# The order of the root, the rounding of the first weight tile and the turns in the normalisations of a two-layer hybrid block

## The chip, the cores and the metric

The kernel runs on one core of one Trainium2 chip. The metric is the time of one execution on the device in microseconds (us). Engines are TensorE (PE, and PEld for its weight loads), VectorE (DVE), ScalarE (ACT), GpSimd (POOL) and SyncE (SP, which issues most transfers).

## The reference

The program computes two layers of a backbone over 512 latent tokens and, as a prefix, 256 context tokens of width 1024. A layer is a token mixer (differential attention, a 2-D Fourier branch and a bidirectional RWKV-7 scan, fed by one input projection, merged by gates) and a channel mixer (ConvGLU). Each of the two begins with a plain layer norm that is then modulated, and its result is multiplied by a weight matrix:

```python
def _ln_plain(x):
    xf = x.astype(jnp.float32)
    mu = jnp.mean(xf, axis=-1, keepdims=True)
    var = jnp.mean(jnp.square(xf - mu), axis=-1, keepdims=True)
    return ((xf - mu) * lax.rsqrt(var + LN_EPS)).astype(x.dtype)

def _modulate(x, shift, scale):
    return _ln_plain(x) * (1.0 + scale) + shift
...
P = _in_proj(_modulate(x, mod[0], mod[1]), ...)           # h @ w_in
f = _conv_ffn(_modulate(x, mod[3], mod[4]), lp)           # u, g = split(h @ ffn_up)
```

The last layer does not need the context tokens in its channel mixer.

## The kernel before

The stream x stays in SBUF, token-major: 128 tokens on the partitions, 1024 features along them, 6 token tiles (4 latent, 2 context). The program is a sequence of stages, each with one instruction list per engine and a barrier at its end; engines order themselves by semaphores within a stage. Products are done in float32 with both operands split in two parts: "hi", the value rounded to the matmul's format, and "lo", the remainder. A product adds hi x hi, hi x lo and lo x hi. Weight tiles of 1024 x 128 (512 KB) are loaded by SyncE into a ring of three (`load_weights`, L312), rounded by ScalarE (`split_hi`, L319, the activation is L325), and their remainder is taken by GpSimd (`split_lo`, L327, L331). SyncE loads tile n when the remainder of tile n - 3 is done.

`norm` (L348) is part of four stages: ahead of the input projection of layer 0 and layer 1 (called from L441: the first and the third normalisation), and ahead of the channel mixer of layer 0 and layer 1 (called from L2134: the second and the fourth). The first three have 6 token tiles, the fourth has 4. It works like this:

- VectorE aggregates the statistics of each token tile (L369; in the first normalisation it takes the statistics themselves too, L364) and adds epsilon (L372). ScalarE takes the root (L400), VectorE the reciprocal (L374) and the product `neg_mean` = -mean/std (L376).
- The rows are normalised token tile by token tile: tiles 0, 1, 3, 4 by VectorE (L378), tiles 2 and 5 by ScalarE (L403). With four tiles these are 0, 1, 3 and 2.
- TensorE turns (transposes) the normalised rows in blocks of 128 x 128 (L393). For feature block j = 0 to 7 it turns this block of all token tiles, into one of three pairs of PSUM banks, and signals `n_T`. It begins when all token tiles are normalised; from block 3 on it waits until the pair of banks has been read.
- ScalarE scales and shifts a turned block out of PSUM (L409, one instruction for the latent and one for the context tokens), from block 3 on when the remainder of block j - 3 is done. GpSimd rounds it (the cast, L417) and VectorE takes the remainder (L382).

Each engine does this ahead of its own part of the stage. The very first things in ScalarE's and GpSimd's lists are the rounding and the remainder of weight tile 0:

```python
            def _(act):
                split_hi(act, sem, rings, 0)
                act.wait_ge(sem("n_var"), 1)
                act.activation(rs[:, 0:nt], rs[:, 0:nt], ACT.Sqrt).then_inc(sem("n_std"), 1)
...
            def _(pool):
                split_lo(pool, sem, rings, 0)
```

After the eight blocks ScalarE rounds weight tile 1 and GpSimd takes its remainder. TensorE, behind its last turn, multiplies weight tile 0 by the activations (`fm_product`, L334, the matmul is L340): for each of the 8 blocks of 128 features three products, of 512 and 256 columns with six tiles and of 512 with four, each block waiting for its remainder (`n_lo`). All further products follow. In the channel mixer two later weight tiles have their remainder taken by VectorE (L2367).

Of the kernel before, what the change touches and what calls it, by code (L numbers as in the profile page):

```python
# [133 lines left out]
def program(nc, A, out):  # L134
    with ExitStack() as top:
# [212 lines left out]
        def norm(sc, block, sem, l, i_shift, i_scale, nt, h, xn, hf, rings, counted):  # L348
# [11 lines left out]
            @block.vector  # L360
            def _(dve):
                for t in range(0 if counted else nt):
                    for f in range(2):
                        i = dve.bn_stats(st_x[:, t, f, :], x[:, t, f * 512:(f + 1) * 512])  # L364
                    i.then_inc(sem("n_stats"), 1)
                for t in range(nt):
                    if not counted:
                        dve.wait_ge(sem("n_stats"), t + 1)
                    i = dve.bn_aggr(mv[:, t, :], st_x[:, t, :, :])  # L369
                i.then_inc(sem("n_mv"), 1)  # L370
                dve.wait_ge(sem("n_mv"), 1)
                dve.tensor_scalar(rs[:, 0:nt], mv[:, 0:nt, 1], LN_EPS, None, ALU.add).then_inc(sem("n_var"), 1)  # L372
                dve.wait_ge(sem("n_std"), 1)
                dve.reciprocal(rs[:, 0:nt], rs[:, 0:nt]).then_inc(sem("n_rstd"), 1)  # L374
                dve.wait_ge(sem("n_rstd"), 1)
                dve.scalar_tensor_tensor(nb[:, 0:nt], mv[:, 0:nt, 0], -1.0, rs[:, 0:nt], ALU.mult, ALU.mult).then_inc(sem("n_nb"), 1)  # L376
                for t in by_dve:
                    dve.tensor_scalar(xn[:, t, :], x[:, t, :], mv[:, t, 0:1], rs[:, t:t + 1],  # L378
                                      ALU.subtract, ALU.mult).then_inc(sem("n_xn"), 1)
                for j in range(KT):  # L380
                    dve.wait_ge(sem("n_hi"), j + 1)
                    dve.tensor_tensor(h[1][:, j, 0:n_tok], hf[:, j % 3, 0:n_tok], h[0][:, j, 0:n_tok].bitcast(F32),  # L382
                                      ALU.subtract).then_inc(sem("n_lo"), 1)

            @block.tensor
            def _(pe):
                pe.wait_ge(sem("n_xn"), len(by_dve))
                pe.wait_ge(sem("n_xa"), len(by_act))
                for j in range(KT):
                    if j >= 3:  # L390
                        pe.wait_ge(sem("n_h"), j - 2)
                    for t in range(nt):
                        m = pe.transpose(bank(2 + 2 * (j % 3), P, t * P), xn[:, t, j * P:(j + 1) * P], ident[:, :])  # L393
                    m.then_inc(sem("n_T"), 1)

            @block.scalar
            def _(act):
                split_hi(act, sem, rings, 0)
                act.wait_ge(sem("n_var"), 1)
                act.activation(rs[:, 0:nt], rs[:, 0:nt], ACT.Sqrt).then_inc(sem("n_std"), 1)  # L400
                act.wait_ge(sem("n_nb"), 1)
                for t in by_act:
                    act.activation(xn[:, t, :], x[:, t, :], ACT.Identity, bias=nb[:, t:t + 1], scale=rs[:, t:t + 1]).then_inc(sem("n_xa"), 1)  # L403
                for j in range(KT):
                    act.wait_ge(sem("n_T"), j + 1)
                    if j >= 3:
                        act.wait_ge(sem("n_lo"), j - 2)
                    for s, (at, n) in enumerate(BOTH if ctx else LAT):
                        m = act.activation(hf[:, j % 3, at:at + n], bank(2 + 2 * (j % 3), n, at), ACT.Identity, bias=sh(j, s), scale=sl(j, s))  # L409
                    m.then_inc(sem("n_h"), 1)  # L410

            @block.gpsimd
            def _(pool):
                split_lo(pool, sem, rings, 0)
                for j in range(KT):
                    pool.wait_ge(sem("n_h"), j + 1)
                    pool.tensor_copy(h[0][:, j, 0:n_tok], hf[:, j % 3, 0:n_tok]).then_inc(sem("n_hi"), 1)  # L417
# [2009 lines left out]
```

## Time and profile before

| | us |
|---|---|
| median of 3 runs | 3760.12 |
| the three runs | 3756.68, 3760.12, 3762.56 |
| the profiled execution, its own time | 3761.08 |
| its span (first to last instruction) | 3758.9 |

TensorE is busy for 3436.3 us of the span, VectorE 1561.3, ScalarE 1263.3 and GpSimd 1081.2; the granted TensorE clock is 0.965 of full speed on average. All starts in the rows below are microseconds from the start of the span. The second column of a timeline row is the time from the start of the first to the end of the last of the instructions merged in it (x4 means four of them); what stands in brackets is the engine's idle time before it and whose signal ended it.

### The profile page before, as it was taken

How to read it: one execution, taken by the hardware profiler on the slowest of the kernel's cores; microseconds unless marked ns; L12 is line 12 of the kernel's file. 1: busy time of each engine (PE TensorE's matmuls, PEld its weight loads, DVE VectorE, ACT ScalarE, POOL GpSimd, SP SyncE). 2: the span in 40 equal slices, each digit the busy share in tenths (PEclk: the TensorE clock that was granted, in tenths of full speed). 3: DMA queues.
4: the chain of work that ended last, by engine and by line, in shares of the span. 5: the costliest groups of instructions: out<-in, count | busy, mean ns of one | idle time of the engine just before them, and what ended most of it. 6: DMA issues, size and time to landing. Idle time of an engine off the chain costs nothing. (4 is left out here: it accounts for less than half of the span.)

```text
span 3758.9 us, 82172 instructions
## 1 busy us (share of the span) xinstructions
PE 3436.3 (91%) x36724; PEld 2756.7 (73%) x36724; DVE 1561.3 (42%) x2341; ACT 1263.3 (34%) x2064; POOL 1081.2 (29%) x649
## 2 busy tenths in 40 slices
PE   5989999999888999799999898999999898969998
PEld 3658888888655777687878666888888666558887
DVE  3233344333177645622112634344443376362224
ACT  3322243333255423221222143234333365223222
POOL 2211132232111412233333232123333113235553
PEclk8989999999999999899999999999999999989999
DMA  6663323342221433133332145334442323433332
GB/s 225 227 196 110 106 77 114 114 127 85 84 85 37 158 115 128 45 129 113 122 119 96 39 144 170 96 109 123 124 121 83 104 90 116 144 95 101 95 96 89
DMA packets 444248, 427.58 MB, mean 114 GB/s; under 512 B 15540, under 2 KB 369002, under 8 KB 436986
## 3 DMA queue, kind: packets, MB, share of 16 engines
q1 hardware_dynamic: 442314, 413.55, 34.9%
q10 hardware_dynamic: 1584, 8.78, 0.6%
q8 instruction: 290, 4.75, 0.5%
q14 instruction: 60, 0.49, 0.0%
HBM read 333.54 MB, written 88.74 MB: 112 GB/s over the span
## 5 line engine op out<-in xcount | busy, mean ns | idle before, releaser
L857 PE MATMUL ps<-I-281_h_hi,I-284_w_hi 128*128 128x256 f32 (+1 forms) x832 | 298.4, 359 | 14.2 <-ACT I-1974_result L1063 9.7
L857 PE MATMUL ps<-I-281_h_hi,I-285_w_lo 128*128 128x256 f32 (+1 forms) x832 | 282.6, 340 | 2.7 <-issue 2.7
L857 PE MATMUL ps<-I-282_h_lo,I-284_w_hi 128*128 128x256 f32 (+1 forms) x832 | 282.9, 340 | 0.0
L2286 POOL TENSOR_TENSOR I-18334_w_lo<-I-18332_w_raw,I-18333_w_hi 128x1024 fp32r<-128x1024 f32 x60 | 145.0, 2416 | 342.5 <-ACT I-18333_w_hi L2249 342.4
L857 PE MATMUL ps<-I-23080_h_hi,I-23083_w_hi 128*128 128x512 f32 (+1 forms) x544 | 213.2, 392 | 13.4 <-ACT I-24473_result L1063 7.8
L857 PE MATMUL ps<-I-23081_h_lo,I-23083_w_hi 128*128 128x512 f32 (+1 forms) x544 | 201.3, 370 | 0.0
L857 PE MATMUL ps<-I-23080_h_hi,I-23084_w_lo 128*128 128x512 f32 (+1 forms) x544 | 200.9, 369 | 0.0
L2286 POOL TENSOR_TENSOR I-38121_w_lo<-I-38119_w_raw,I-38120_w_hi 128x1024 fp32r<-128x1024 f32 x60 | 144.2, 2404 | 154.4 <-ACT I-38120_w_hi L2249 154.4
L857 PEld LDWEIGHTS ps<-I-281_h_hi,I-284_w_hi 128*128 128x128 f32 x832 | 158.8, 191 | 39.0 <-ACT I-1974_result L1063 9.9
L340 PE MATMUL ps<-I-18329_h_hi,I-18333_w_hi 128*128 128x512 f32 x704 | 183.1, 341 | 1.0 <-DVE I-18330_h_lo L382 1.0
L821 POOL TENSOR_TENSOR I-285_w_lo<-I-283_w_raw,I-284_w_hi 128x1024 fp32r<-128x1024 f32 x34 | 82.3, 2421 | 353.4 <-ACT I-284_w_hi L1081 353.4
L2249 ACT ACTIVATE I-18333_w_hi<-I-18332_w_raw 128x1024 fp32r<-128x1024 f32 x61 | 64.6, 1059 | 354.7 <-PE ps L340 234.9
L340 PE MATMUL ps<-I-18329_h_hi,I-18334_w_lo 128*128 128x512 f32 x704 | 182.1, 340 | 0.0
L340 PE MATMUL ps<-I-18330_h_lo,I-18333_w_hi 128*128 128x512 f32 x704 | 180.1, 337 | 0.0
L857 PEld LDWEIGHTS ps<-I-281_h_hi,I-285_w_lo 128*128 128x128 f32 x832 | 159.0, 191 | 17.7
L821 POOL TENSOR_TENSOR I-23084_w_lo<-I-23082_w_raw,I-23083_w_hi 128x1024 fp32r<-128x1024 f32 x34 | 84.8, 2494 | 297.0 <-ACT I-23083_w_hi L1081 297.0
L857 PEld LDWEIGHTS ps<-I-282_h_lo,I-284_w_hi 128*128 128x128 f32 x832 | 159.3, 191 | 14.2
L1063 ACT ACTIVATE I-1974_result<-ps 128x512 f32<-128x512 f32 x104 | 51.1, 493 | 340.1 <-PE ps L857 340.0
L340 PE MATMUL ps<-I-38116_h_hi,I-38120_w_hi 128*128 128x512 f32 x352 | 137.6, 391 | 1.8 <-DVE I-38117_h_lo L382 1.8
L340 PE MATMUL ps<-I-38116_h_hi,I-38121_w_lo 128*128 128x512 f32 x352 | 137.0, 389 | 0.0
L340 PE MATMUL ps<-I-38117_h_lo,I-38120_w_hi 128*128 128x512 f32 x352 | 137.0, 389 | 0.0
L918 PEld LDWEIGHTS ps<-I-49_x 64*64 64x64 f32 x3840 | 116.8, 135 | 21.6 <-issue 12.6
(892 smaller groups left out, 8826.3 us busy)
## 6 DMA issues: line engine op xcount, KB each, us to landing
I-283_w_raw<-in_w_in SPq DMA_DIRECT2D x67, 512.0 KB, 6.1
I-23082_w_raw<-in_w_in SPq DMA_DIRECT2D x67, 512.0 KB, 5.1
I-18342_ada_w<-in_ada_w SPq DMA_DIRECT2D x24, 1024.0 KB, 5.9
I-18332_w_raw<-in_ffn_up SPq DMA_DIRECT2D x44, 512.0 KB, 3.9
I-38119_w_raw<-in_ffn_up SPq DMA_DIRECT2D x44, 512.0 KB, 3.9
proj_d<-I-1974_result SPq DMA_DIRECT2D x52, 384.0 KB, 2.8
I-482_ada_w<-in_ada_w SPq DMA_DIRECT2D x16, 1024.0 KB, 5.6
I-18332_w_raw<-in_ffn_down SPq DMA_DIRECT2D x22, 512.0 KB, 3.3
```

Of the source, the lines that this page charges most:

```text
L340: m = pe.matmul(dst[:, at:at + n], w[wi][:, k, :], a[ai][:, k, at:at + n], start=k == 0 and i == 0, stop=k == kt - 1 and i == 2)
L821: pool.tensor_tensor(lo(s), raw(s), hi(s).bitcast(F32), ALU.subtract).then_inc(sem("w_lo"), 1)
L857: m = pe.matmul(bank(6 + i % 2, n_c), w[:, k, :], hv[:, k, c0:c0 + n_c], start=k == 0 and v == 0, stop=k == KT - 1 and v == 2)
L918: m = pe.matmul(side(ps[rows(i), (4 + d) * 512 + c0:(4 + d) * 512 + c0 + C], n_lv, d), NAT[d][rows(1 - i), c0:c0 + C], side(T[d][rows(1 - ...
L1063: act.activation(res[:, s % 2, c0:c0 + n_c], bank(6 + i % 2, n_c), ACT.Copy, scale=DH_A ** -0.5 if J_Q <= slots[s][0] < J_K else 1.0).then ...
L2249: act.activation(pair(g)[0], rings[0][:, g % 3, :, :], ACT.Copy).then_inc(sem("w_hi"), 1)
L2286: pool.tensor_tensor(pair(g)[1], rings[0][:, g % 3, :, :], pair(g)[0].bitcast(F32), ALU.subtract).then_inc(sem("w_lo"), 1)
```

## The change

In `norm`, ScalarE takes the root and normalises its token tiles first, and rounds weight tile 0 after that. The remainder of weight tile 0 moves from the head of GpSimd's list to VectorE's, behind its normalised rows and ahead of the remainders of the activations. TensorE turns the first three feature blocks token tile by token tile (tile 0, 2, 1, 5, 3, 4 with six tiles; 0, 2, 1, 3 with four), waiting for each tile by itself, and signals the three blocks with the turns of the last token tile; blocks 3 to 7 are turned as before.

```diff
@@ -377,6 +377,7 @@
                 for t in by_dve:
                     dve.tensor_scalar(xn[:, t, :], x[:, t, :], mv[:, t, 0:1], rs[:, t:t + 1],
                                       ALU.subtract, ALU.mult).then_inc(sem("n_xn"), 1)
+                split_lo(dve, sem, rings, 0)
                 for j in range(KT):
                     dve.wait_ge(sem("n_hi"), j + 1)
                     dve.tensor_tensor(h[1][:, j, 0:n_tok], hf[:, j % 3, 0:n_tok], h[0][:, j, 0:n_tok].bitcast(F32),
@@ -384,23 +385,31 @@
 
             @block.tensor
             def _(pe):
-                pe.wait_ge(sem("n_xn"), len(by_dve))
-                pe.wait_ge(sem("n_xa"), len(by_act))
-                for j in range(KT):
-                    if j >= 3:
-                        pe.wait_ge(sem("n_h"), j - 2)
+                turn = lambda j, t: pe.transpose(bank(2 + 2 * (j % 3), P, t * P), xn[:, t, j * P:(j + 1) * P], ident[:, :])
+                order = sorted(range(nt), key=lambda t: (by_act if t in by_act else by_dve).index(t))
+                for t in order:
+                    if t in by_act:
+                        pe.wait_ge(sem("n_xa"), by_act.index(t) + 1)
+                    else:
+                        pe.wait_ge(sem("n_xn"), by_dve.index(t) + 1)
+                    for j in range(3):
+                        m = turn(j, t)
+                        if t == order[-1]:
+                            m.then_inc(sem("n_T"), 1)
+                for j in range(3, KT):
+                    pe.wait_ge(sem("n_h"), j - 2)
                     for t in range(nt):
-                        m = pe.transpose(bank(2 + 2 * (j % 3), P, t * P), xn[:, t, j * P:(j + 1) * P], ident[:, :])
+                        m = turn(j, t)
                     m.then_inc(sem("n_T"), 1)
 
             @block.scalar
             def _(act):
-                split_hi(act, sem, rings, 0)
                 act.wait_ge(sem("n_var"), 1)
                 act.activation(rs[:, 0:nt], rs[:, 0:nt], ACT.Sqrt).then_inc(sem("n_std"), 1)
                 act.wait_ge(sem("n_nb"), 1)
                 for t in by_act:
                     act.activation(xn[:, t, :], x[:, t, :], ACT.Identity, bias=nb[:, t:t + 1], scale=rs[:, t:t + 1]).then_inc(sem("n_xa"), 1)
+                split_hi(act, sem, rings, 0)
                 for j in range(KT):
                     act.wait_ge(sem("n_T"), j + 1)
                     if j >= 3:
@@ -411,7 +420,6 @@
 
             @block.gpsimd
             def _(pool):
-                split_lo(pool, sem, rings, 0)
                 for j in range(KT):
                     pool.wait_ge(sem("n_h"), j + 1)
                     pool.tensor_copy(h[0][:, j, 0:n_tok], hf[:, j % 3, 0:n_tok]).then_inc(sem("n_hi"), 1)
```

## Rows read from the trace of the kernel before

**Rows 1.** The page, part 1: busy time, share of the span, instructions.

```profile
PE 3436.3 (91%) x36724; PEld 2756.7 (73%) x36724; DVE 1561.3 (42%) x2341; ACT 1263.3 (34%) x2064; POOL 1081.2 (29%) x649
```

**Rows 2.** The chain that ended last: start, duration (us), what.

```profile
3371.60 1.06 ACT I-38120_w_hi L325
...
3372.99 2.09 DVE I-38136_neg_mean L376
...
3390.43 11.86 PE ps L340 x51
```

**Rows 3.** Timeline of ScalarE, second normalisation: start, duration, what, [idle before <- releaser].

```profile
1543.46 1.06 ACT L325 ACTIVATE I-18333_w_hi<-I-18332_w_raw 128x1024 fp32r<-128x1024 f32 x1 [8.76 <-DMA I-18332_w_raw<-in_ffn_up]
...
1546.99 2.37 ACT L403 ACTIVATE I-18336_x_norm<-I-49_x,I-18350_neg_mean,I-18349_rstd 128x1024 f32<-128x1024 f32 x2 [2.37 <-DVE I-18350_neg_mean L376]
1551.48 4.76 ACT L409 ACTIVATE I-18337_h_f<-ps,I-63_mod 128x512 f32<-128x512 f32 x8 [2.12 <-PE ps L393]
```

**Rows 4.** Timeline of VectorE, second normalisation.

```profile
1539.94 0.17 DVE L372 TENSOR_SCALAR I-18349_rstd<-I-18348_mean_var 128x6 f32<-128x6 f32 x1
...
1544.88 2.08 DVE L376 SCALAR_TENSOR_TENSOR I-18350_neg_mean<-I-18348_mean_var,I-18349_rstd 128x6 f32<-128x6 f32 x1
1546.88 2.97 DVE L378 TENSOR_SCALAR I-18336_x_norm<-I-49_x,I-18348_mean_var,I-18349_rstd 128x1024 f32<-128x1024 f32 x4
```

**Rows 5.** Timeline of GpSimd, second normalisation.

```profile
1544.60 2.34 POOL L331 TENSOR_TENSOR I-18334_w_lo<-I-18332_w_raw,I-18333_w_hi 128x1024 fp32r<-128x1024 f32 x1 [47.83 <-ACT I-18333_w_hi L325]
```

**Rows 6.** Timeline of TensorE, second normalisation.

```profile
1549.90 6.15 PE L393 MATMUL ps<-I-50_ident,I-18336_x_norm 128*128 128x128 f32 x36 [23.80 <-DVE I-18336_x_norm L378]
```

**Rows 7.** Timelines of ScalarE, then VectorE, first normalisation.

```profile
46.37 1.28 ACT L400 ACT_TABLE_LOAD   x1
...
54.28 6.20 ACT L409 ACTIVATE I-290_rv_raw<-ps,I-63_mod 128x512 f32<-128x512 f32 x10 [2.12 <-PE ps L393]
...
48.92 0.17 DVE L372 TENSOR_SCALAR I-298_rstd<-I-297_mean_var 128x6 f32<-128x6 f32 x1
...
49.59 0.17 DVE L376 SCALAR_TENSOR_TENSOR I-299_neg_mean<-I-297_mean_var,I-298_rstd 128x6 f32<-128x6 f32 x1
49.67 2.97 DVE L378 TENSOR_SCALAR I-287_k_and_kk<-I-49_x,I-297_mean_var,I-298_rstd 128x1024 f32<-128x1024 f32 x4
```

**Rows 8.** Timelines of ScalarE, then VectorE, third normalisation.

```profile
2161.33 1.06 ACT L325 ACTIVATE I-23083_w_hi<-I-23082_w_raw 128x1024 fp32r<-128x1024 f32 x1 [9.12 <-DMA I-23082_w_raw<-in_w_in]
...
2169.35 4.76 ACT L409 ACTIVATE I-23089_rv_raw<-ps,I-64_mod 128x512 f32<-128x512 f32 x8 [2.12 <-PE ps L393]
...
2157.49 0.17 DVE L372 TENSOR_SCALAR I-23097_rstd<-I-23096_mean_var 128x6 f32<-128x6 f32 x1
```

**Rows 9.** Timelines of ScalarE, then VectorE, fourth normalisation.

```profile
3378.46 3.34 ACT L409 ACTIVATE I-38124_h_f<-ps,I-64_mod 128x512 f32<-128x512 f32 x4 [2.10 <-PE ps L393]
...
3368.12 0.17 DVE L372 TENSOR_SCALAR I-38135_rstd<-I-38134_mean_var 128x4 f32<-128x4 f32 x1
```

**Rows 10.** Lines 378, 393, 2367, 417: count, duration in ns min/median/max, first and last start.

```profile
L378 DVE TENSOR_SCALAR I-287_k_and_kk<-I-49_x,I-297_mean_var,I-298_rstd x4: 806/806/807, 49.7 to 51.8; 128x1024 f32<-128x1024 f32 x4
...
L393 PEld LDWEIGHTS ps<-I-50_ident,I-287_k_and_kk x48: 138/226/229, 52.7 to 61.0; 128*128 128x128 f32 x48
...
L2367 DVE TENSOR_TENSOR I-18334_w_lo<-I-18332_w_raw,I-18333_w_hi x1: 1219/1219/1219, 2095.4 to 2095.4; 128x1024 fp32r<-128x1024 f32 x1
...
L417 POOL CAST I-38116_h_hi<-I-38124_h_f x8: 609/892/1156, 3379.3 to 3386.3; 128x512 fp32r<-128x512 f32 x8
```

**Rows 11.** Stretches: length, busy us (count) of each engine, PEclk, DMA share, GB/s.

```profile
1550.00:1553.00 3.00, 3.00 (x15) 3.00 (x16) 0.00 (x0) 1.47 (x3) 0.22 (x1) 0.50 0.03 9
...
1556.00:1559.00 3.00, 1.67 (x14) 1.39 (x14) 3.00 (x3) 2.02 (x4) 2.04 (x3) 1.00 0.02 5
```

**Rows 12.** Timeline of TensorE, end of the first normalisation and first product.

```profile
70.50 0.62 PE L340 MATMUL ps<-I-281_h_hi,I-284_w_hi 128*128 128x512 f32 x2 [1.72 <-DVE I-282_h_lo L382]
...
73.35 1.01 PE L340 MATMUL ps<-I-281_h_hi,I-284_w_hi 128*128 128x512 f32 x2
```


## The prediction

> **What bounds the kernel now.** I read the page first: TensorE is busy for 91% of the span [rows 1], so a microsecond is worth something only where TensorE stands still or where everything waits ahead of it. The chain that ended last is read next. It runs through one of the four normalisations, and there not through TensorE: rounding of the first weight tile, root, reciprocal, a 6-element or 4-element product that takes 2.09 us, the normalised rows, turns, then the long product at 3390.43 [rows 2]. Then I read the timelines of ScalarE, VectorE, GpSimd and TensorE in each normalisation. In the second one (before the channel mixer of layer 0) VectorE has the variances at 1539.94 + 0.17, but ScalarE takes no root: its first job is the rounding, which waits for the weights until 1543.46 [rows 3, 4]. The reciprocal follows, then neg_mean, whose 2.08 us end just as GpSimd's remainder of the weight tile does (1544.60 + 2.34 = 1546.94) [rows 4, 5]. Only at 1546.88 does the first normalised row start, and TensorE's first turn at 1549.90 [rows 4, 6]. The third and the fourth look alike [rows 8, 9]. The first is different: the weights were there early, neg_mean took 0.17 us and the statistics on VectorE set the pace [rows 7].
>
> So what ends last ahead of the normalised rows is, three times in four, the weight DMA, then ScalarE's rounding, then GpSimd's remainder. All that follows the first scaled block (I call its start on ScalarE S, and measure each normalisation by it) is a fixed chain of scale, cast on GpSimd, remainder on VectorE, eight times, to the last eighth of the first product: in the first normalisation it starts at 70.50, 16.2 us after S = 54.28, in the fourth at 3390.43, 12.0 us after S = 3378.46 [rows 2, 7, 9, 12]. After that TensorE runs with hardly a gap. I take the change in S as the change in time, and then correct for what it does to the chain behind it.
>
> **The root ahead of the rounding.** Nothing stands before it on ScalarE. In the first normalisation, where ScalarE was waiting, the step from the start of the variance (48.92) to the start of the first normalised row (49.67) is 0.75 us, root, reciprocal and neg_mean included [rows 7]. The same step gives 1539.94 + 0.75 = 1540.69 in the second (was 1546.88), 2157.49 + 0.75 = 2158.24 in the third and 3368.12 + 0.75 = 3368.87 in the fourth [rows 4, 8, 9]. This needs both halves of the edit: the order on ScalarE removes the wait for the weights, and the remainder leaving GpSimd removes the 1.9 us by which neg_mean was too long.
>
> **The turns by token tile.** The first row takes 0.80 us [rows 10]; TensorE began 0.05 us after the last row's end [rows 4, 6]. The clock it is granted there is 0.50 of full speed, 1.2 GHz [rows 11], after an idle stretch, and then a turn is issued every 0.23 us [rows 10]. Six turns to the first scaled block took 1551.48 - 1549.90 = 1.58 us [rows 3, 6]. In the new order block 0 of the last token tile is the 16th turn of 18, so S is 1.58 + 10 x 0.228 = 3.86 us after the first turn. Four rows take 2.97 us on VectorE (one every 0.72) and two 2.37 us on ScalarE [rows 3, 4], 18 turns need 4.1 us, so TensorE is never starved and sets the pace. Before, S came 2.97 us of rows plus 1.58 + 0.05 after their start; now it comes 0.80 + 0.05 + 3.86. That is 4.60 against 4.71: **at this clock the new order of the turns by itself is worth nothing** in a six-tile normalisation. With four tiles it is the tenth turn, 1.58 + 4 x 0.228 = 2.49 us.
> S is the later of this and of ScalarE coming free from the rounding, which now stands behind its rows (2.37 us, begun 0.11 us after VectorE's [rows 3, 4]):
> - first: first turn 49.67 + 0.85 = 50.52, S = 54.38; ScalarE free at about 52.2 + 1.06 = 53.2. Was 54.28: 0.1 lost.
> - second: 1541.54, S = 1545.40; ScalarE free at 1543.46 + 1.06 = 1544.5. Was 1551.48: 6.1 won.
> - third: 2159.09, S = 2162.95; ScalarE free at 2162.4. Was 2169.35: 6.4 won [rows 8].
> - fourth: 3369.72 + 2.49 = 3372.2, but the rounding runs 3371.60 to 3372.6 [rows 2], so S = 3372.6. Was 3378.46: 5.9 won.
>
> **The remainder on VectorE.** 1.22 us where VectorE does this operation today, against 2.34 on GpSimd [rows 5, 10]. It starts when the rounding ends and lies in time in which VectorE waits for the first cast, due 1.3 us after S with six tiles: it is over at 1545.8 against 1546.7 in the second, and earlier in the others. Cost nothing; without that cover 1.22 each. In the fourth it doesn't fit: it would run 3372.7 to 3373.9, and the first cast is due at 3372.6 + 0.8. Casts there take from 0.61 to 1.16 us [rows 10], the long ones beside VectorE's remainders. The cost lies between 0 and the whole 1.2 us; I take the middle, 0.6, which is nearest to the lengthening of those casts, and since cast and remainder alternate to the end of the chain I charge all of it. The Trainium skill, SBUF — State Buffer, "Who interferes with whom", says that a VectorE instruction with two SBUF inputs and a GpSimd one that reads SBUF take turns, the second to start blocked for the whole of the first. Rows 4 and 5 agree, and it speaks against this move: by it the cast waits from 3373.4 to 3373.9 and nothing else waits, and the sum would be 17.8.
>
> **Queues.** SyncE's fourth weight load waits for the first remainder. In the second to fourth normalisation it leaves a little sooner, in the first some 5.7 us later (54.5 for 48.8), but its tile is rounded only once the second tile's product is over, which can't begin before 70.50 [rows 12]: nothing. GpSimd has nothing before its first cast. Waits per token tile on TensorE: nothing visible when already met; bound 0.2 each. The table load for the root ran at 46.37, ahead of the wait for the variance [rows 7], so it moves into idle time; if it came behind that wait it costs 1.28 in the first normalisation (bounds 0 and 1.28, I take 0).
>
> **Sum**: -0.1 + 6.1 + 6.4 + 5.9 - 0.6 = **17.7 us** off 3761.08, the profiled execution's own time (span 3758.9). The median of the three runs is 0.96 lower, and 3760.12 - 17.7 = **3742.4 us**.
>
> **What the clock may take.** TensorE now does 18 turns, stops for about 1 us until the first scaled block is out, and does the rest in groups of six as banks come free. Before, it turned from 1549.90 for 6.15 us without a stop, and the clock rose within that time [rows 6, 11]. If it rises later, groups of six take 1.4 us where scaled blocks come every 1.2 to 1.5, and part of the first product runs at half speed, where two matmuls take 1.01 for 0.62 us [rows 12]. TensorE waited 1.72 us for the last remainder in the first normalisation [rows 12], which hides the first 3 us of that. Bounds 0 and 1.3 each; I take 0.
>
> **Rivals.**
> 1. *The turns are fast enough*: the clock is up early or turns are issued faster, and ScalarE's rounding sets S. Then 1.0 + 7.0 + 7.0 + 5.9 = 20.9, less 0.6: time **3739.8**. Against it, 229 ns a turn in all four at their start. Chance 0.12.
> 2. *neg_mean stays long*, its 2.08 us belonging to something other than GpSimd's remainder: 3 x 1.9 = 5.7 less, **3748.1**. Against it, 0.17 us in the first. Chance 0.05.
> 3. *The clock is late by a lot, slower than before*. With stops between the groups TensorE keeps 1.2 GHz into the first product. At full clock 51 matmuls 512 wide took 11.86 us [rows 2], so the first product of six tiles, worth 36 of them, takes 8.4, and 16.8 at half clock; less the 1.7 hidden that is up to 6.7 each, 27 in all: 3742.4 + 27 = **3769**. It decides from 4.4 us lost each, which is 12 us of product at half clock in each of the four. For it: the drop at 73.35 after a stop and a thin stretch [rows 12]. Against it: from 1556 to 1559 TensorE was busy with turns for 1.67 of 3 us, and the clock stayed at 1.00 [rows 11]. Chance 0.03. The Trainium skill, TensorE: Matmul & The Clock Gate, "A second HAM failure mode: psum-queue depth-cycling", tells of short idles between groups that made the clock swing; no row here shows it in these turns, and by it this rival's 3769 would be the time.
> 4. *Given back or not effective*: the 17.7 us are taken up by a later wait on a transfer, or the first rows are held by something else: **3756 to 3760**. Against it: TensorE hardly waits after the first product, and loads follow its progress. Chance 0.05.
>
> My own case, part of the clock's price included (3740 to 3747), has 0.75.
>
> **How the numbers follow.** The three runs spread by 5.9 us. 0.2% (7.5 us) is about what a measurement of this kernel can tell from no change. Range: down to rival 1 less half of that spread, 3737; up to 3742.4 + 4 x 1.3 for the clock + half the spread, 3750, which takes in rival 2. Faster by over 0.2% (under 3752.6): 0.75 + 0.12 + 0.05, and a part of rival 4 = 0.93; same 0.04; slower 0.03.
>
> **What would show it.** Right: root 0.03 us after the variance in all four; neg_mean 0.17 us; rows from 0.75 us after the variance's start; TensorE's first turn 1.6 us after that start; S at 3.86 us after the first turn, at 1.2 GHz; the remainder on VectorE 1.2 us and no idle of GpSimd's casts on it except in the fourth; 16 us (12 in the fourth) from S to the last eighth. Wrong: a table load behind the variance, S held by ScalarE's rounding with six tiles, a longer way from S to the last eighth, matmuls of the first product at half clock, or a wait that is new behind it.

## The result, and the profile of the changed kernel

Four runs of the changed kernel gave a median of 3735.44 us (3734.16 to 3740.24), four of the kernel before 3760.26; the ratio is 0.9937, 95% interval 0.992 to 0.9954. Forecast were 3742.4 us and a range from 3737 to 3750: the time lies 1.6 us under the range, and 24.8 us were won where 17.7 were forecast. Three later comparisons of the same two kernels, with five or six runs of the changed one each, gave 3738.05 against 3757.98 (ratio 0.9952, 0.9939 to 0.9966), 3741.35 against 3757.45 (0.9950, 0.9932 to 0.9969) and 3733.31 against 3752.21 (0.9947, 0.9933 to 0.9961): 19.9, 16.1 and 18.9 us won. The interval of the first ratio, 0.992 to 0.9954, takes in the later ratios, and also the forecast one (3742.4 / 3760.12 = 0.9953): four runs against four do not tell 25 us from 18. The record names another chip for each of the three later comparisons, and in the last one both kernels are 5 to 8 us faster, so a difference is best read within one comparison. What is to be explained is therefore twofold: a gain of 18 to 19 us, and 6 us more in the first comparison.

The page of the changed kernel's first profile:

```profile
span 3733.1 us, 82168 instructions
...
PE 3431.3 (92%) x36724; PEld 2749.0 (74%) x36724; DVE 1558.0 (42%) x2345; ACT 1262.9 (34%) x2064; POOL 1074.0 (29%) x645
```

The span is 25.8 us shorter than before. TensorE is busy for 3431.3 us, 5.0 us less than before [rows 1], although it does the same 36724 matmuls: a first sign that not all of the gain is waiting removed. Stage by stage those 5 us are not in the normalisations: there TensorE is busy for 1298.4 us (1296.7 before), elsewhere for 2132.9 (2139.6 before). In the second profiles of the two kernels it is the other way round, 3435.1 us changed and 3428.6 before, so it does not belong to the change. Then the timelines of the second normalisation, ScalarE, VectorE, GpSimd and TensorE (start, time, what, the idle time before and its releaser):

```profile
1534.99 0.21 ACT L408 ACTIVATE I-18353_rstd<-I-18353_rstd 128x6 f32<-128x6 f32 x1 [5.44 <-DVE I-18353_rstd L372]
1535.65 2.38 ACT L411 ACTIVATE I-18340_x_norm<-I-49_x,I-18354_neg_mean,I-18353_rstd 128x1024 f32<-128x1024 f32 x2 [0.46 <-DVE I-18354_neg_mean L376]
1538.19 1.06 ACT L325 ACTIVATE I-18337_w_hi<-I-18336_w_raw 128x1024 fp32r<-128x1024 f32 x1 [0.16 <-DMA I-18336_w_raw<-in_ffn_up]
1539.80 4.62 ACT L418 ACTIVATE I-18341_h_f<-ps,I-63_mod 128x512 f32<-128x512 f32 x8 [0.55 <-PE ps L388]
...
1534.78 0.17 DVE L372 TENSOR_SCALAR I-18353_rstd<-I-18352_mean_var 128x6 f32<-128x6 f32 x1
...
1535.45 0.17 DVE L376 SCALAR_TENSOR_TENSOR I-18354_neg_mean<-I-18352_mean_var,I-18353_rstd 128x6 f32<-128x6 f32 x1
1535.53 2.98 DVE L378 TENSOR_SCALAR I-18340_x_norm<-I-49_x,I-18352_mean_var,I-18353_rstd 128x1024 f32<-128x1024 f32 x4
1539.28 1.23 DVE L331 TENSOR_TENSOR I-18338_w_lo<-I-18336_w_raw,I-18337_w_hi 128x1024 fp32r<-128x1024 f32 x1 [0.77 <-ACT I-18337_w_hi L325]
1541.96 0.96 DVE L383 TENSOR_TENSOR I-18334_h_lo<-I-18341_h_f,I-18333_h_hi 128x768 fp32r<-128x768 f32 x1 [1.45 <-POOL I-18333_h_hi L425]
1543.63 12.17 DVE L383 TENSOR_TENSOR I-18334_h_lo<-I-18341_h_f,I-18333_h_hi 128x768 fp32r<-128x768 f32 x7 [0.72 <-POOL I-18333_h_hi L425]
...
1541.10 0.83 POOL L425 CAST I-18333_h_hi<-I-18341_h_f 128x768 fp32r<-128x768 f32 x1 [49.52 <-ACT I-18341_h_f L418]
...
1536.40 3.58 PE L388 MATMUL ps<-I-50_ident,I-18340_x_norm 128*128 128x128 f32 x18 [15.52 <-DVE I-18340_x_norm L378]
1541.08 0.88 PE L388 MATMUL ps<-I-50_ident,I-18340_x_norm 128*128 128x128 f32 x6 [1.11 <-ACT I-18341_h_f L418]
...
1555.86 0.61 PE L340 MATMUL ps<-I-18333_h_hi,I-18337_w_hi 128*128 128x512 f32 x2 [0.99 <-DVE I-18334_h_lo L383]
```

Against [rows 3 to 6]: the root runs 0.04 us after the variance's end, neg_mean takes 0.17 us, the rows start 0.75 us after the variance's start. The rounding waits for the weights only 0.16 us, behind ScalarE's rows. The remainder takes 1.23 us on VectorE, which then waits 1.45 us for the first cast. TensorE's first turn comes 1.62 us after the variance's start, the first scaled block at 1539.80, 5.02 us after it; before it was 11.54 (1551.48 - 1539.94). From the first scaled block to the last eighth of the product (1555.86) are 16.1 us, as before.

The clock in that stretch (length, busy us of each engine, granted clock, DMA share, GB/s):

```profile
1536.00:1540.00 4.00, 3.58 (x18) 3.29 (x18) 3.23 (x5) 3.29 (x4) 0.00 (x0) 0.59 1.13 301
...
1544.00:1547.00 3.00, 1.51 (x12) 1.07 (x11) 3.00 (x3) 1.88 (x4) 2.19 (x3) 1.00 0.02 5
```

It rose to 2.4 GHz while the 18 first turns were still running, so they took 3.58 us (4.10 where it did not rise). In the second profile of the same kernel it did not, and there the first scaled block comes at 5.33 us (1536.09 - 1530.76):

```profile
1536.09 4.61 ACT L418 ACTIVATE I-18341_h_f<-ps,I-63_mod 128x512 f32<-128x512 f32 x8 [0.64 <-PE ps L388]
...
1530.76 0.17 DVE L372 TENSOR_SCALAR I-18353_rstd<-I-18352_mean_var 128x6 f32<-128x6 f32 x1
```

The fourth normalisation, VectorE's timeline and then the chain of waits, answers to [rows 2, 9]:

```profile
3347.95 0.17 DVE L372 TENSOR_SCALAR I-38147_rstd<-I-38146_mean_var 128x4 f32<-128x4 f32 x1
...
3352.47 1.23 DVE L331 TENSOR_TENSOR I-38133_w_lo<-I-38131_w_raw,I-38132_w_hi 128x1024 fp32r<-128x1024 f32 x1 [1.53 <-ACT I-38132_w_hi L325]
...
3351.38 1.06 ACT I-38132_w_hi L325
3352.43 0.68 ACT I-38136_h_f L418
...
3353.17 1.00 POOL I-38128_h_hi L425
...
3354.20 1.08 DVE I-38129_h_lo L383
...
3364.49 11.88 PE ps L340 x51
```

Here the weights come last, as forecast: rounding 3351.38 to 3352.43, first scaled block behind it, remainder of the weight tile at 3352.47 for 1.23 us. The first scaled block comes at 4.39 us (3352.34 on ScalarE's timeline, less 3347.95); the forecast had 4.48.

For all profiles I took the same distances, in us from the start of the variance to the first scaled block (S) and to the start of the last eighth of the first product (E), from the starts of these instructions:

| profile | first S, E | second S, E | third S, E | fourth S, E |
|---|---|---|---|---|
| before | 5.36, 21.58 | 11.54, 27.61 | 11.87, 27.93 | 10.34, 22.30 |
| before, again | 5.36, 21.43 | 11.32, 27.55 | 11.40, 27.62 | 10.45, 22.41 |
| changed | 5.33, 21.39 | 5.02, 21.08 | 4.96, 21.02 | 4.39, 16.54 |
| changed, again | 5.33, 21.40 | 5.33, 21.42 | 5.33, 21.42 | 4.60, 16.76 |
| changed, third | 5.33, 21.39 | 5.33, 21.40 | 5.33, 21.37 | 4.59, 16.75 |
| changed, fourth | 5.33, 21.39 | 5.29, 21.36 | 5.12, 21.18 | 4.51, 16.66 |

And the lengths of stages, in us from one barrier (L123) to the next:

| profile | the four with a normalisation | all else |
|---|---|---|
| before | 212.3 + 617.5 + 170.8 + 391.3 = 1391.9 | 2366.5 |
| before, again | 210.5 + 617.5 + 171.1 + 391.4 = 1390.5 | 2360.3 |
| changed | 210.7 + 611.0 + 164.1 + 385.6 = 1371.4 | 2361.1 |
| changed, again | 210.3 + 611.3 + 164.9 + 385.8 = 1372.3 | 2362.4 |
| changed, third | 210.5 + 611.3 + 164.8 + 385.8 = 1372.5 | 2367.2 |
| changed, fourth | 210.6 + 611.3 + 164.6 + 385.7 = 1372.2 | 2357.7 |

The stages with a normalisation repeat within 1.1 us from profile to profile of the changed kernel. All else, in which no line was changed, ranges over 9.5 us within that one kernel. (Stages and all else together lack about half a microsecond of each span.)

### The profile page after: what moved, and what is told of

The parts are those of the page before. It is cut to its first block and busy times, and to the rows that moved or that the text cites. A ratio compares the mean times of both kernels' runs of the same rounds, so it can differ in the third digit from the quotient of the medians.

```text
span 3733.1 us, 82168 instructions
## 1 busy us (share of the span) xinstructions
PE 3431.3 (92%) x36724; PEld 2749.0 (74%) x36724; DVE 1558.0 (42%) x2345; ACT 1262.9 (34%) x2064; POOL 1074.0 (29%) x645
## 5 line engine op out<-in xcount | busy, mean ns | idle before, releaser
L865 PE MATMUL ps<-I-281_h_hi,I-284_w_hi 128*128 128x256 f32 (+1 forms) x832 | 298.6, 359 | 16.1 <-ACT I-1978_result L1071 8.7
L2294 POOL TENSOR_TENSOR I-18338_w_lo<-I-18336_w_raw,I-18337_w_hi 128x1024 fp32r<-128x1024 f32 x60 | 145.0, 2416 | 342.5 <-ACT I-18337_w_hi L2257 342.3
L865 PE MATMUL ps<-I-23088_h_hi,I-23091_w_hi 128*128 128x512 f32 (+1 forms) x544 | 212.4, 390 | 12.0 <-ACT I-24485_result L1071 7.5
L865 PE MATMUL ps<-I-23089_h_lo,I-23091_w_hi 128*128 128x512 f32 (+1 forms) x544 | 200.5, 369 | 0.8 <-issue 0.8
L865 PE MATMUL ps<-I-23088_h_hi,I-23092_w_lo 128*128 128x512 f32 (+1 forms) x544 | 200.1, 368 | 0.0
L2294 POOL TENSOR_TENSOR I-38133_w_lo<-I-38131_w_raw,I-38132_w_hi 128x1024 fp32r<-128x1024 f32 x60 | 144.4, 2407 | 154.7 <-ACT I-38132_w_hi L2257 154.7
L340 PE MATMUL ps<-I-18333_h_hi,I-18337_w_hi 128*128 128x512 f32 x704 | 183.1, 341 | 1.0 <-DVE I-18334_h_lo L383 1.0
L340 PE MATMUL ps<-I-18333_h_hi,I-18338_w_lo 128*128 128x512 f32 x704 | 182.1, 340 | 0.0
L340 PE MATMUL ps<-I-18334_h_lo,I-18337_w_hi 128*128 128x512 f32 x704 | 180.1, 337 | 0.0
L340 PE MATMUL ps<-I-38128_h_hi,I-38132_w_hi 128*128 128x512 f32 x352 | 137.8, 392 | 1.2 <-DVE I-38129_h_lo L383 1.2
L340 PE MATMUL ps<-I-38129_h_lo,I-38132_w_hi 128*128 128x512 f32 x352 | 137.0, 389 | 0.0
```

The source lines that it names most:

```text
L340: m = pe.matmul(dst[:, at:at + n], w[wi][:, k, :], a[ai][:, k, at:at + n], start=k == 0 and i == 0, stop=k == kt - 1 and i == 2)
L865: m = pe.matmul(bank(6 + i % 2, n_c), w[:, k, :], hv[:, k, c0:c0 + n_c], start=k == 0 and v == 0, stop=k == KT - 1 and v == 2)
L2294: pool.tensor_tensor(pair(g)[1], rings[0][:, g % 3, :, :], pair(g)[0].bitcast(F32), ALU.subtract).then_inc(sem("w_lo"), 1)
```

## The experiments

**The changed kernel once more**, no edit.

> The changed kernel once more. The forecast was 3742.4 us and the four runs gave 3735.4; by the traces the four normalisation stages became 20.5 us shorter and the other stages 5.3 us shorter, where nothing was changed. If the 5.3 us were chance of one profiled run (theory N), a second profile has them elsewhere or not at all, and the median of new runs lies nearer 3740. If they belong to the changed kernel, by the clock that TensorE is granted in the later stages (theory K), it stays within 2 us of 3735.4 and the same stages are shorter again.

Measured 3738.05 us (3735.38 to 3748.35, six runs), 19.9 under the kernel before of the same comparison, whose 17 runs ran from 3751.9 to 3768.86. The stages without a normalisation were again shorter than in the first profile of before, by 4.1 us, but not the same ones: the attention stage of layer 0, from 1010.8 to 1224.0 before, by 5.8 us (first profile of the changed kernel: 2.8), the layer-1 scan longer by 1.5 (first profile: shorter by 3.1). That speaks for theory N; the median, 2.6 us up from 3735.4, decides nothing by itself.

**The turns as before, everything else changed.**

```diff
-                for t in order:
-                    ...
-                    for j in range(3):
-                        m = turn(j, t)
+                pe.wait_ge(sem("n_xn"), len(by_dve))
+                pe.wait_ge(sem("n_xa"), len(by_act))
+                for j in range(KT):
+                    if j >= 3:
+                        pe.wait_ge(sem("n_h"), j - 2)
+                    for t in range(nt):
+                        m = pe.transpose(...)
```

> The changed kernel with TensorE's turns as before (all rows first, then block by block). Own theory: first scaled block 5.35 us after the variance's start with six tiles, against 5.0 to 5.4 with turns by tile; about 1 us slower in all than the changed kernel, 3736 to 3737. Rival: the turns by tile carry the 7 us that the forecast missed; then 3742.

Measured 3739.32 us (ratio to before 0.9949, 0.9936 to 0.9963). VectorE's variance, ScalarE's scaled blocks and TensorE's turns in the second normalisation:

```profile
1538.08 0.17 DVE L372 TENSOR_SCALAR I-18349_rstd<-I-18348_mean_var 128x6 f32<-128x6 f32 x1
...
1543.45 4.86 ACT L410 ACTIVATE I-18337_h_f<-ps,I-63_mod 128x512 f32<-128x512 f32 x8 [0.89 <-PE ps L394]
...
1541.87 6.24 PE L394 MATMUL ps<-I-50_ident,I-18336_x_norm 128*128 128x128 f32 x36 [17.69 <-DVE I-18336_x_norm L378]
```

First scaled block at 1543.45 - 1538.08 = 5.37 us, its four stages 1372.1 us. Turning by token tile gives 5.33. The turns carry nothing of the gain.

**The turns by token tile alone**, on the kernel before (the diff's part for TensorE and nothing else).

> The kernel before with the turns by token tile alone. Own theory: 0 to 2 us faster than before, 3758 to 3760. Rival, turns carry the missing 7 us: 3753. If the clock of the later stages depends on where they start (theory K), up to 6 us either way with the normalisation stages unchanged.

Measured 3757.72 us over eleven runs (ratio 0.9998, 0.9989 to 1.0006): no change. First scaled block at 11.18, 11.18 and 10.20 us in the second to fourth normalisation, 0.1 to 0.7 sooner than in the two profiles of before; the four stages together 1390.1 us against 1390.5 in the second profile of before.

**ScalarE's order alone**; remainder on GpSimd, turns as before.

```diff
             def _(act):
-                split_hi(act, sem, rings, 0)
                 act.wait_ge(sem("n_var"), 1)
...
+                split_hi(act, sem, rings, 0)
                 for j in range(KT):
                     act.wait_ge(sem("n_T"), j + 1)
```

> The kernel before with ScalarE's order alone changed; the remainder of the weight tile stays on GpSimd and the turns as before. The prediction said that neg_mean stays 2 us long unless the remainder leaves GpSimd. On a second reading the remainder then starts after the rounding, 3 us behind neg_mean: neg_mean should take 0.17 us, and GpSimd's remainder (2.34 us) makes the first cast late by about 0.5 in the second and third and 1.7 us in the fourth normalisation. So 3 us more than without the turns: about 3739 to 3740. By the text of the prediction 5.7 us more: 3742.

Measured 3741.47 us (ratio 0.9952, 0.9939 to 0.9965), the four stages 1375.4 us: 3.3 more than without the turns. neg_mean in the second and the fourth normalisation (ns, min/median/max), then GpSimd and ScalarE in the fourth:

```profile
L376 DVE SCALAR_TENSOR_TENSOR I-18350_neg_mean<-I-18348_mean_var,I-18349_rstd x1: 165/165/165, 1531.8 to 1531.8; 128x6 f32<-128x6 f32 x1
...
L376 DVE SCALAR_TENSOR_TENSOR I-38136_neg_mean<-I-38134_mean_var,I-38135_rstd x1: 163/163/163, 3346.0 to 3346.0; 128x4 f32<-128x4 f32 x1
...
3350.37 2.37 POOL L331 TENSOR_TENSOR I-38121_w_lo<-I-38119_w_raw,I-38120_w_hi 128x1024 fp32r<-128x1024 f32 x1 [35.28 <-ACT I-38120_w_hi L325]
3352.68 2.19 POOL L417 CAST I-38116_h_hi<-I-38124_h_f 128x512 fp32r<-128x512 f32 x3
...
3350.20 2.10 ACT L409 ACTIVATE I-38124_h_f<-ps,I-64_mod 128x512 f32<-128x512 f32 x3
```

neg_mean is short with the remainder still on GpSimd, because that now starts only after the rounding. GpSimd works on it from 3350.37 for 2.37 us, so the first cast starts at 3352.68, 2.48 us behind the first scaled block (3350.20) instead of 0.8. From S to E are 13.45 us there against 12.14 without the turns, and S is 0.27 later; in the second and third it is 0.2 and 0.4 in E. That makes 2.2 of the 3.3 us; where the rest comes in was not followed. The order alone brings 15 of the 18 us.

**The remainder on VectorE alone.**

```diff
             def _(pool):
-                split_lo(pool, sem, rings, 0)
...
+                split_lo(dve, sem, rings, 0)
                 for j in range(KT):
                     dve.wait_ge(sem("n_hi"), j + 1)
```

> The kernel before with the remainder of weight tile 0 on VectorE behind its rows, ScalarE's order and the turns as before. neg_mean should take 0.17 us for 2.08, so the rows start 1.9 us earlier in the second to fourth normalisation and each of these stages is 1.9 us shorter: 5.7 us faster than before in all. Rival: neg_mean is short but the remainder now delays the first cast or the first remainder of the activations; then 2 to 4 us.

Measured 3756.23 us over twelve runs (ratio 0.9986, 0.9973 to 0.9999). The median is 1.2 us under that of before, the mean 4.2, and the ratio stands for 5.3. VectorE in the second normalisation, and GpSimd's first cast:

```profile
1534.11 0.17 DVE L372 TENSOR_SCALAR I-18349_rstd<-I-18348_mean_var 128x6 f32<-128x6 f32 x1
...
1538.97 0.17 DVE L376 SCALAR_TENSOR_TENSOR I-18350_neg_mean<-I-18348_mean_var,I-18349_rstd 128x6 f32<-128x6 f32 x1
1539.05 2.98 DVE L378 TENSOR_SCALAR I-18336_x_norm<-I-49_x,I-18348_mean_var,I-18349_rstd 128x1024 f32<-128x1024 f32 x4
1541.94 1.22 DVE L331 TENSOR_TENSOR I-18334_w_lo<-I-18332_w_raw,I-18333_w_hi 128x1024 fp32r<-128x1024 f32 x1
...
1544.96 0.82 POOL L417 CAST I-18329_h_hi<-I-18337_h_f 128x768 fp32r<-128x768 f32 x1 [54.06 <-ACT I-18337_h_f L410]
```

neg_mean takes 0.17 us, the weight tile's remainder 1.22, and the cast comes 1.8 us after that has ended. E is 25.66, 25.92 and 20.28 us, that is 1.9, 1.7 and 2.1 less than in the second profile of before: the mechanism as expected. Stage by stage 1.9, 1.7 and 0.5 us came out, and all else took 2371.2 us, the longest of all profiles. So the expected 5.7 are there at the end of the normalisations, 4.1 of them in the lengths of the stages (the fourth loses 1.6 again behind its first product, and why was not followed). The execution times bound the gain only between 0.4 and 10 us, which takes in both.

**The kernel before once more**, no edit.

> The kernel before once more, to have a second profile and its own spread. Theory N (what the stages without a normalisation take varies from execution to execution): these stages differ from the first profile by several us in places that the code gives no reason for, while the second to fourth normalisation stages repeat within 0.3 us; the first normalisation stage comes out 1.5 us shorter than in the first profile, as in every run since. Theory K (the clock in later stages belongs to the kernel): all stages repeat.

Measured 3757.00 us over twelve runs (3750.88 to 3765.05), ratio to the other runs of before 0.9995 (0.9984 to 1.0006). The first normalisation stage is 1.8 us shorter than in the profile that the forecast used, the others within 0.3. The attention stage of layer 0, in the first and in the second profile of the same kernel (length, busy us and count of TensorE, its weight loads, VectorE, ScalarE, GpSimd, granted clock, DMA share, GB/s):

```profile
1010.84:1223.96 213.12, 174.35 (x1040) 118.60 (x1040) 147.44 (x296) 115.59 (x250) 23.75 (x50) 0.92 0.22 72
```

```profile
1011.31:1218.33 207.02, 167.26 (x1040) 113.44 (x1040) 147.52 (x296) 115.49 (x250) 23.75 (x50) 0.96 0.23 74
```

The same 1040 matmuls, 213.1 us at a mean clock of 0.92 and 207.0 at 0.96, with VectorE's and ScalarE's busy times equal to 0.1 us. TensorE needs 7.1 us more for the same matmuls, and the stage is 6.1 us longer. This is theory N, and in this stage it has a cause: the granted clock. Over all thirteen profiles the time of the unchanged stages and the time that they had at 1.2 GHz go together with a correlation of 0.81; lengths scatter by 4.8 us (standard deviation), and by 2.9 about the line, so part of the variation is left over.

**The changed kernel a third time.**

> The changed kernel a third time. By its stages it should be 18 us faster than the kernel before of the same call (17.7 forecast, 18.3 by the second to fourth normalisation stages of two profiles). If the 24.8 us of the first four runs were the true gain, 25.

Measured 3741.35 us, 16.1 under before; the ratio, 0.9950, stands for 18.8.

**TensorE kept busy ahead of the first rows.**

```diff
+                for i in range(12 if counted else 34):
+                    pe.transpose(bank(0, P, i % 4 * P), ident[:, :], ident[:, :])
                 for t in order:
```

> The changed kernel with dummy turns of the identity on TensorE (34 in the first, 12 in the other normalisations) while it waits for the first rows. Theory: TensorE's 1.2 GHz sets the first scaled block. If the dummies lift the clock, 16 turns take 2.3 us for 3.9, and the first scaled block comes at about 4.4 us after the variance's start (the last row and ScalarE's rounding then set it) instead of 5.0 to 5.4: 2 to 3 us off the changed kernel in all. If they don't lift it in time: no change, or up to 1 us slower each where dummies are still running when the first row is ready.

Measured 3750.35 us over twelve runs (ratio 0.9981, 0.9968 to 0.9994): 9 us slower than the changed kernel in the same comparison. In the second normalisation, TensorE, ScalarE, and the clock from 1537 to 1540:

```profile
1535.93 2.80 PE L391 MATMUL ps<-I-50_ident 128*128 128x128 f32 x12 [13.25 <-PEq L123]
1538.52 3.83 PE L388 MATMUL ps<-I-50_ident,I-18374_x_norm 128*128 128x128 f32 x18
...
1541.25 1.06 ACT L325 ACTIVATE I-18371_w_hi<-I-18370_w_raw 128x1024 fp32r<-128x1024 f32 x1 [1.47 <-DMA I-18370_w_raw<-in_ffn_up]
1542.21 4.14 ACT L420 ACTIVATE I-18375_h_f<-ps,I-63_mod 128x512 f32<-128x512 f32 x7
```

```profile
1537.00:1540.00 3.00, 3.00 (x16) 3.00 (x15) 2.97 (x6) 2.38 (x2) 0.00 (x0) 0.50 1.00 279
```

In this normalisation the dummies ran 0.4 us into the time of the first turns, TensorE was busy without a stop, and its clock was still 0.50; S came at 5.68, the weights being late as well (rounding at 1541.25, 4.7 us after the variance). In the third the clock was at 0.50 for the first turns too and rose while they ran, with S at 5.28. In the first, with 34 of them, the clock did rise (1.00 from 49 to 52.3, while TensorE waited for the rows) and the first turns ran at 2.4 GHz; but from 53.8 to 57 it was 0.50 again, with turns running, and S came at 5.09 instead of 5.33. In the fourth it rose during the first turns, and S, which the rounding sets there, stayed at 4.39. The four stages took 1373.5 us, 1.0 to 2.1 more than in the profiles of the changed kernel. So no six-tile normalisation had all its first turns at the high clock, and the forecast gain of that case was not tested. Of the 9 us the profiles show 4.0 (spans 3744.3 and 3740.3): 1.0 in the four stages and 2.9 in the unchanged ones (2370.1 against 2367.2). Where the rest lies no profile shows.

**Two dummies only.**

```diff
-                for i in range(12 if counted else 34):
+                for i in range(2):
```

> The changed kernel with two dummy turns of the identity at the head of TensorE's list in each normalisation. With 34 and 12 of them twelve runs had a median of 3750 us, though the four normalisation stages were only 1.2 us longer than in the changed kernel. If that came from the dummies' work, two of them cost nothing and the median is that of the changed kernel (3738 to 3741). If any shift of TensorE's instruction list does it, it lies again near 3750. If it was scatter, anything between.

Measured 3739.89 us over nine runs (3728.51 to 3750.41), against 3733.31 for the changed kernel in the same comparison (ratios to before 0.9963, 0.9948 to 0.9978, and 0.9947, 0.9933 to 0.9961, which overlap); four stages 1372.2 us, S and E within 0.1 us of those of the changed kernel. Between the two answers: it does not say whether a shifted instruction list makes the later stages slower or whether nine runs scattered so. This stays open.

**The changed kernel a fourth time.**

> The changed kernel a fourth time, for the distribution. 18 to 19 us faster than the kernel before, within the 2 us that medians of such runs still scatter by; the four normalisation stages together 1371 to 1373 us, as in three profiles so far (before: 1392 and 1390).

Measured 3733.31 us, 18.9 under before; four stages 1372.2.

**Only feature block 0 by token tile.**

```diff
-                    for j in range(3):
-                        m = turn(j, t)
-                        if t == order[-1]:
-                            m.then_inc(sem("n_T"), 1)
-                for j in range(3, KT):
-                    pe.wait_ge(sem("n_h"), j - 2)
+                    m = turn(0, t)
+                m.then_inc(sem("n_T"), 1)
+                for j in range(1, KT):
+                    if j >= 3:
+                        pe.wait_ge(sem("n_h"), j - 2)
```

> The changed kernel, but only feature block 0 is turned token tile by token tile; blocks 1 to 7 follow block by block. Theory: with six tiles the first scaled block waits for 16 turns at 1.2 GHz behind the first row. Now it waits for one turn behind the last row: 0.75 + 2.97 + 0.05 + 0.44 = 4.2 us after the variance's start, and ScalarE is free of the rounding at 4.2 to 4.5. So 4.5 instead of 5.33 (5.0 where the clock rose early), 0.8 us in each of three normalisations, nothing in the fourth: 2.4 us less than the changed kernel in the stages, which the execution times can hardly show. Rival: block 1 or 2 is then turned too late and the scaled blocks stall by as much; then the last eighth of the first product starts as before, 21.4 us after the variance's start.

Measured 3733.17 us (3728.11 to 3737.84), ratio to before 0.9946 (0.9931 to 0.9962), against 3733.31 for the changed kernel. VectorE's variance, ScalarE and TensorE in the second normalisation:

```profile
1530.76 0.17 DVE L372 TENSOR_SCALAR I-18353_rstd<-I-18352_mean_var 128x6 f32<-128x6 f32 x1
...
1534.19 1.06 ACT L325 ACTIVATE I-18337_w_hi<-I-18336_w_raw 128x1024 fp32r<-128x1024 f32 x1 [0.19 <-DMA I-18336_w_raw<-in_ffn_up]
1535.16 4.90 ACT L417 ACTIVATE I-18341_h_f<-ps,I-63_mod 128x512 f32<-128x512 f32 x8
...
1532.37 1.24 PE L388 MATMUL ps<-I-50_ident,I-18340_x_norm 128*128 128x128 f32 x3 [15.48 <-DVE I-18340_x_norm L378]
1534.06 6.93 PE L388 MATMUL ps<-I-50_ident,I-18340_x_norm 128*128 128x128 f32 x39 [0.44 <-ACT I-18340_x_norm L410]
...
1551.22 0.62 PE L340 MATMUL ps<-I-18333_h_hi,I-18337_w_hi 128*128 128x512 f32 x2 [0.99 <-DVE I-18334_h_lo L383]
```

The first scaled block starts at 1535.16, 4.40 us after the variance, directly behind the rounding, which now sets it. S is 4.30, 4.40 and 4.29 us with six tiles, E 20.42, 20.47 and 20.52, each 0.9 to 1.0 us sooner than at S = 5.33. The first three stages together are 2.0 to 2.8 us shorter than in the four profiles of the changed kernel. The fourth came out 1.5 us longer with its E unchanged at 16.58, which stays unexplained, so the stages' sum, 1371.1, is only 0.3 to 1.4 us less, and the execution times can't tell the two apart. As a mechanism it is shown; as a faster kernel it is not.

## Why the prediction was right, and where it was wrong

**The chain ahead of the rows** was read rightly. The step of 0.75 us from the variance to the rows held in all four; the weights stopped setting the rows. One slip in it is small: the rounding of the fourth normalisation ends at 3371.60 + 1.06 = 3372.66, so that term should have read 5.8 and not 5.9.

**"This needs both halves of the edit"** was wrong. With ScalarE's order alone neg_mean took 0.165 us, since GpSimd's remainder moves behind it by itself. With the remainder alone it took 0.17 us too. Each half removes neg_mean's 1.9 us; only the order removes the wait for the weights. Rival 2, neg_mean staying long, fell in every run that removed the overlap; where it stayed (turns alone) neg_mean kept its 2.08 us.

**The turns** were forecast as worth nothing at 1.2 GHz, and are: 5.33 against 5.37. The first scaled block was forecast 5.46 us after the variance and came at 5.33, 3.71 after the first turn and not 3.86. The forecast took 0.228 us from one turn to the next, which is the length of a weight load [rows 10]. The starts of single turns at 1.2 GHz lie 0.213 us apart, and 1.58 + 10 x 0.213 = 3.71. The row of the 18 first turns of the changed kernel says the same: less the last turn's own 0.42 us they fill 3.68 us in 17 steps.

```profile
52.76 4.10 PE L388 MATMUL ps<-I-50_ident,I-287_k_and_kk 128*128 128x128 f32 x18 [10.63 <-DVE I-287_k_and_kk L378]
```

Rival 1 came true in part: with the clock up during the first turns S was 5.02 and 4.96 in two normalisations of one profile and 5.12 in one of another. TensorE still set it, not the rounding.

**The remainder on VectorE** cost nothing with six tiles. In the fourth normalisation the term of 0.6 us was mis-sized: from S to E the way grew from 11.96 to between 12.14 and 12.16 us, 0.2. The first cast was lengthened (1.00 us for 0.61), but that did not travel to the end. The last remainder of the activations ends only after GpSimd's remainder of weight tile 1, which started 9.01 us after S before and 9.03 after the change.

**A wait of the same kind stands at the end of the chain**, in both kernels, and neither the prediction nor a run took it up. GpSimd and then VectorE at the end of the fourth normalisation before:

```profile
3387.47 2.36 POOL L2286 TENSOR_TENSOR I-38121_w_lo<-I-38119_w_raw,I-38120_w_hi 128x1024 fp32r<-128x1024 f32 x1
...
3387.54 2.83 DVE L382 TENSOR_TENSOR I-38117_h_lo<-I-38124_h_f,I-38116_h_hi 128x512 fp32r<-128x512 f32 x1 [0.51 <-POOL I-38116_h_hi L417]
```

The last remainder of the activations takes 2.83 us where the shortest of that size took 0.68, and the last eighth of the product waits for it (3390.43). With six tiles it takes 3.1 us for 0.96, before and after. These are some 2 us in each normalisation, an estimate from these durations; that moving the second weight tile's remainder would win them is not shown.

**Sum by normalisation**, from E in the second profile of before to the four of the changed kernel: 0.0 (forecast 0.1 lost), 6.1 to 6.5 (6.1), 6.2 to 6.6 (6.4), 5.7 to 5.9 (5.3). From the first profile of before, which the forecast was worked out on, they are 0.2, 6.2 to 6.5, 6.5 to 6.9 and 5.5 to 5.8. By stages 1391.2, the mean of two, less 1372.1, the mean of four: 19.1 us, of which 0.9 come from the one long first stage in the profile of before. Forecast 17.7. The medians of the later comparisons gave 16.1 to 19.9.

**The clock after the stop between the turns** (bounds 0 to 1.3 each, taken as 0) and rival 3 behind it: S to E stayed 16.1 us with TensorE busy for only 1.51 of 3 us between turns, at a clock of 1.00. In the first normalisation of the changed kernel the clock stayed at 0.50 from 57 to 61 in the first profile and was 1.00 from 56.5 to 59.5 in the second, at about the same distance from the variance, and E was 21.39 and 21.40: a late rise cost nothing there. Rival 3 did not appear. Rival 4, a gain given back, did not either.

**The step that failed** is "The three runs spread by 5.9 us", and the half of it that went into the range. It took three executions as the kernel's scatter, and it gave the stages that the edit does not touch no term at all, so the starting value of 3760.12 and the difference of two small medians had a margin of 2.95 us together. What the runs showed in its place: 46 further runs of before, in two comparisons, go from 3751.1 to 3769.5, 18 us, and the unchanged stages differ by 9.5 us between four profiles of one kernel. The change itself was forecast right within 1.5 us (17.7 against 18 to 19). Later medians of before were 3758.0, 3757.5 and 3752.2, so 3760.3 stood at the upper side, and the changed kernel's 3735.4 stood under the 3738.1 and 3741.4 of the first two of these comparisons (3733.3 in the third); that the chips differ limits what these medians say.

In the two first profiles it can be seen. Of 25.8 us of span, 20.5 are in the four stages with a normalisation. Of these 1.6 are in the first, whose E moved by 0.2 alone. Four stages in which nothing changed gave 2.8, 2.3, 3.1 and 2.1, and the remaining stages gave some back, so the unchanged ones make 5.4 together. That the time came out under the range was therefore, as far as these profiles show, chance of the executions that were drawn. Much of the variation goes with the granted clock, which is shown for the attention stage and a correlation for the rest; why the clock falls in a given execution and not in another I did not settle. That one part of it belongs to the kernel's form rather than to chance (the runs with dummies point there) stays open too.

## What to carry to other kernels

Look for the engine whose first instruction of a stage waits for a transfer that nothing needs yet; what stands behind it pays for the transfer, and moving it behind the work that is ready brought 15 of 18 us here. Before counting a finer hand-over as a gain, count the pieces on the engine that hands over at the clock that it has just after being idle: 16 turns behind the first row took as long as waiting for all rows and doing six. And before giving a range for a time, get the spread of the unchanged stages from more than one profile; for a change of half a per cent the lengths of the changed stages, which repeated within 1.1 us here, tell more than four executions do.

## What the runs showed of the hardware

- A VectorE instruction on 6 elements per partition, 0.17 us alone, took 2.08 us beside a GpSimd subtraction of 128 x 1024 with inputs in SBUF and ended with it (1546.96 and 1546.94). In the fourth normalisation of the changed kernel it is GpSimd's cast that is longer, 1.00 us for 0.61, beside VectorE's subtraction. The Trainium skill, SBUF — State Buffer, "Who interferes with whom", says that the later of two such instructions is blocked for the whole of the first. The trace agrees for the 6 elements. The cast ended 0.47 us after the subtraction (3354.17 and 3353.70).
- The same program's stage of 1040 matmuls took 213.1 us at a mean granted clock of 0.92 and 207.0 at 0.96. The 29 executions of the kernel before in one comparison went from 3751.1 to 3769.5 us, and the stages without a normalisation took from 2357.7 to 2367.2 us in the four profiles of the changed kernel.
- At 1.2 GHz block turns of 128 x 128 started 0.21 us apart, at 2.4 GHz 0.11. In the second normalisation of the changed kernel the clock was 1.00 from 1544 to 1547 with TensorE busy for 1.51 of 3 us.
- The table load for the root ran ahead of the wait for the variance, at the head of ScalarE's list (at 43.38 in the first profile of the changed kernel, the variance at 51.14), and cost nothing in the first normalisation. The other three have none there.
